# The tail of a four-head mixer stage: one projection moved up, one product moved back, one projection interleaved with broadcasts

## What is computed

```python
z = h @ w_in                               # columns: conv (x_c, B, C), q, k, v, o, gates
u = cg * xc                                # conv group, 512 channels, 4 tiles of 128
conv = w_conv[0]*full[:, 0:L] + w_conv[1]*full[:, 1:L+1] + w_conv[2]*full[:, 2:L+2]
y_conv = bg * conv
num = w_inter * (q C) + s v                # mLSTM, 4 heads of 128; s = (q k) * decay
den = w_inter * (q n) + sum(s)
h = num / max(|den|, exp(-mt))
C_new = w_old * C + sum(w_s k v)           # new state, an output; n_new alike
y = concat([group_rmsnorm(y_conv, 8), group_rmsnorm(sigmoid(o) * h, 4)]) @ w_out
x = x + gt1 * y
```

## Time and profile before

| | |
|---|---|
| median of three runs | 1788.6 us |
| runs | 1797.53, 1788.6, 1786.57 us |
| profiled execution | 1797.36 us, its span 1795.6 us |
| PE busy, share of the span | 1698.9 us, 95% |
| DVE, POOL, ACT busy | 1196.6, 1129.9, 666.7 us |
| mean granted TensorE clock | 0.976 of 2.4 GHz |

### The profile page before, as it was taken

The page is one execution under the profiler, slowest core; times in us unless marked ns, Lnnn a source line. Parts: engine busy times, 40 slices in busy tenths (PEclk is TensorE's granted clock), DMA queues, the critical chain, the costliest instruction groups (busy, mean ns, idle before and its releaser), DMA issues.

```text
span 1795.6 us, 27306 instructions
## 1 busy us (share of the span) xinstructions
PE 1698.9 (95%) x10559; PEld 1622.5 (90%) x10559; DVE 1196.6 (67%) x2286; ACT 666.7 (37%) x1063; POOL 1129.9 (63%) x676
## 2 busy tenths in 40 slices
PE   7999999798999999999999989888999999999996
PEld 3899887696999999999998989878999999999996
DVE  4341244625776799997777768455788787878855
ACT  2454232233334333323333333334444444444442
POOL 1667222031335897766666656586898899999862
PEclk9999999799999999999999999999999999999998
DMA  7545131224305888779998999999999999999961
GB/s 265 208 143 169 61 102 69 66 77 135 106 14 157 266 281 280 217 265 329 309 346 294 339 309 306 334 380 334 383 405 401 369 400 405 405 404 402 400 217 62
DMA packets 196737, 467.57 MB, mean 260 GB/s; under 512 B 21120, under 2 KB 103040, under 8 KB 196480
## 3 DMA queue, kind: packets, MB, share of 16 engines
q1 hardware_dynamic: 82176, 245.46, 38.8%
q0 software_dynamic: 46080, 167.79, 24.8%
q10 hardware_dynamic: 68352, 52.57, 9.0%
HBM read 410.78 MB, written 54.97 MB: 259 GB/s over the span
## 4 chain that ended last, share of the span: by engine, by line
PE 73%; DVE 10%; DMA 5%; ACTq 3%; POOL 3%; issue 3%; ACT 2%; SPq 0%; DVEq 0%; POOLq 0%
PE ps L886 41%; PE ps L672 18%; PE ps L897 4%; ACTq L1184 3%; PE ps L692 2%; DMA tab<-in_tab 2%; POOL tLo L630 2%; DMA ug<-in_urows,eidx 1%; DVE ug L1503 1%; PE ps L701 1%; POOL ug L640 1%; DVE best L1612 1%; PE ps L861 1%; DVE eqa L1605 1%; DVE eqb L1608 1%
## 5 line engine op out<-in xcount | busy, mean ns | idle before, releaser
L630 POOL TENSOR_TENSOR tLo<-tab,tHi 128x1024 fp32r<-128x1024 f32 x256 | 624.3, 2440 | 207.5 <-ACT tHi L1131 204.6
L886 PE MATMUL ps<-hHi,tLo 128*128 128x384 f32 x1024 | 357.0, 349 | 20.9 <-POOL tLo L630 13.7
L1131 ACT CAST tHi<-tab 128x1024 fp32r<-128x1024 f32 x256 | 268.3, 1048 | 290.1 <-PE ps L886 166.5
L886 PE MATMUL ps<-actHi,tLo 128*128 128x384 f32 x1024 | 343.1, 335 | 7.6 <-POOL tLo L630 4.2
L886 PE MATMUL ps<-hHi,tHi 128*128 128x384 f32 x1024 | 349.5, 341 | 0.0
L886 PE MATMUL ps<-hLo,tHi 128*128 128x384 f32 x1024 | 348.3, 340 | 0.0
L886 PE MATMUL ps<-actLo,tHi 128*128 128x384 f32 x1024 | 342.1, 334 | 0.0
L886 PE MATMUL ps<-actHi,tHi 128*128 128x384 f32 x1024 | 342.1, 334 | 0.0
L618 POOL TENSOR_TENSOR wLo<-raw,wHi 128x1024 fp32r<-128x1024 f32 x53 | 127.8, 2411 | 310.2 <-ACT wHi L967 310.2
L1503 DVE SCALAR_TENSOR_TENSOR ug<-ug,ps 128x1024 f32<-128x1024 f32 x160 | 192.1, 1218 | 88.0 <-DMA ug<-in_urows,eidx 86.7
L886 PEld LDWEIGHTS ps<-hHi,tLo 128*128 128x128 f32 x1024 | 196.4, 192 | 24.0 <-ACT ga L1181 14.6
(11 more groups left out here) (342 smaller groups left out, 2498.2 us busy)
## 6 DMA issues: line engine op xcount, KB each, us to landing
tab<-in_tab SPq DMA_DIRECT2D x256, 512.0 KB, 7.1
raw<-in_w SPq DMA_DIRECT2D x101, 512.0 KB, 3.9
gelu_scratch<-ga ACTq DMA_DIRECT2D x128, 192.0 KB, 5.0
gate_scratch<-stage ACTq DMA_DIRECT2D x12, 2048.0 KB, 17.8
gt<-gate_scratch SPq DMA_DIRECT2D x32, 768.0 KB, 7.7
gin<-gelu_scratch SPq DMA_DIRECT2D x128, 192.0 KB, 10.5
ug<-in_urows,eidx POOLq DMA_INDIRECT x160, 6.8
ug<-in_vrows,eidx POOLq DMA_INDIRECT x160, 7.7
```

What stands on the lines that cost most here:

```text
L630: pool.tensor_tensor(tLo[:, n % SPL], tab[:, n % TABS], tHi[:, n % SPL].bitcast(F32), ALU.subtract).then_inc(s_tlo, 1)
L886: last = mm(ps[:, bank, 0:TD], w, x[:, k, 0:TD], start=first, stop=end)
L1131: nc.scalar.copy(tHi[:, n % SPL], tab[:, n % TABS]).then_inc(s_thi, 1)
```

## The change

Three things are changed, and what hangs on them. First, in the table, units 26, 27 and 28 stand one place earlier: 26 behind the denominator of head 2, 27 behind its state product, 28 behind the transposes of head 3, and nothing in head 3 behind that. On DVE `conv(3)` moves from behind the weighted scores to ahead of the masks. Second, head 3's state product leaves its place behind the denominator, so that `group_sum(3)` follows the denominator; it now stands behind unit 29, in other banks, and its update on DVE behind the second residual of the output projection. Third, only two broadcasts stand ahead of unit 29; the other six stand inside it, broadcast k + 2 ahead of the matmuls of tile k, in two bank pairs in turn. The two small copies `cp` and `cs` move behind the sum of squares.

```diff
-AFTER_T, AFTER_S, AFTER_D, AFTER_ST = ([17, 21, 24, 27], [18, 22, 25, 28], [19, None, None, None], [20, 23, 26, None])
+AFTER_T, AFTER_S, AFTER_D, AFTER_ST = ([17, 21, 24, 28], [18, 22, 25, None], [19, None, 26, None], [20, 23, 27, None])
...
-            s = 2 * i if i < 2 else 4 + 2 * (i % 2)
+            s = 6 * (i % 2)
             return ps[:, s:s + 2, 0:HF]
...
-            def unit(n, free, made=None):
+            def unit(n, free, made=None, ahead=None):
...
                 for k in range(KT):
+                    if ahead is not None and k + 2 < KT:
+                        ahead(k + 2)
                     if made is not None:
                         pe.wait_ge(s_hlo, made + k + 1)
...
+            def group_rows_out(i):
+
+                if i >= 2:
+                    pe.wait_ge(s_y, i - 1)
+                rows = slice(0, 8) if i < CT else slice(32, GR)
+                for x in (grHi, grLo):
+                    for h in range(2):
+                        last = mm(bcast_pair(i)[:, h], bselr[rows, i % 4, :], x[rows, h * HF:(h + 1) * HF],
+                                  start=(x is grHi), stop=(x is grLo))
+                last.then_inc(s_gbc, 1)
...
+                if h < NH - 1:
+                    state_product(h, 2, (3, 4))
                 conv_unit(AFTER_ST[h])
 
             pe.wait_ge(s_ev, U_OUT)
             group_sum(NH - 1)
 
             pe.wait_ge(s_glo, 1)
+            group_rows_out(0)
+            group_rows_out(1)
+            unit(U_OUT, U_OUT, KT, group_rows_out)
+            pe.wait_ge(s_y, CT + NH)
+            state_product(NH - 1, 6, (4, 5))
+            for n in range(U_OUT + 1, U_PQ):
+                unit(n, max(n - 1, U_OUT))
             pe.wait_ge(s_stc, NH)
...
+                if h == NH - 1:
+                    conv(h)
                 v.wait_ge(s_ex, h + 1)
...
+                if k == 1:
+                    state_update(NH - 1, 6, (4, 5))
```

More of the change, by code:

```diff
@@ L763, in group_sum, with state_product @@
                 last.then_inc(s_gst, 1)
+            def state_product(h, small_bank, banks):
+                pe.wait_ge(s_vw, h + 1)
+                pe.wait_ge(s_hm, h + 1)
+                for i in range(NH):
+                    mm(ps[:, small_bank, 0:DH + 1], ktok[:, i, :], vw[:, i, :], start=(i == 0), stop=(i == NH - 1))
+                mm(ps[:, small_bank, 136:136 + NB], ktok[0:TS, NH, :], wsm[:], start=True, stop=True)
+                for i, b in enumerate(banks):
+                    last = mm(ps[:, b, :], ktok[0:TS, NH, :], vsm[:, 4 * i:4 * i + 4, :], start=True, stop=True)
+                last.then_inc(s_stp, 1)
+            def group_rows_out(i):
[7 more added lines that the diff above has]
+                last.then_inc(s_gbc, 1)
             for h in range(NH):
@@ L825, in _ @@
             pe.wait_ge(s_glo, 1)
-            pe.wait_ge(s_stc, NH)
[L827 to L837, removed]
+            group_rows_out(0)
[5 more added lines that the diff above has]
+                unit(n, max(n - 1, U_OUT))
+            pe.wait_ge(s_stc, NH)
             mod_rows(NMS)
@@ L1404, in group_add, with state_update @@
                 v.sem_inc(s_gacc, 1)
+            def state_update(h, small_bank, banks):
+                tt(nso[:, h], n0[:, h], wib[:, h, TS:TS + NB], ALU.mult)
+                link(tt(csb[:], csb[:], over(wib[:, h, TS:TS + NB], DH), ALU.mult))
+                v.wait_ge(s_stp, h + 1)
+                tt(csb[:, 0:4], csb[:, 0:4], ps[:, banks[0], :].rearrange("p (b d) -> p b d", b=4), ALU.add)
+                nc.vector.tensor_copy(cst[:, h], ps[:, small_bank, 0:DH])
+                nc.vector.tensor_copy(npo[:, h:h + 1], ps[:, small_bank, DH:DH + 1])
+                tt(nso[:, h], nso[:, h], ps[:, small_bank, 136:136 + NB], ALU.add)
+                tt(csb[:, 4:8], csb[:, 4:8], ps[:, banks[1], :].rearrange("p (b d) -> p b d", b=4), ALU.add).then_inc(s_stc, 1)
             for h in range(NH):
@@ L1443, in _ @@
                 v.wait_ge(s_den, h + 1)
[L1444 to L1453, removed]
+                last = tt(drow[32:GR, TP:T], drow[32:GR, TP:T], ps[32:GR, 5, 288:288 + TS], ALU.add)
                 if h < NH - 1:
+                    state_update(h, 2, (3, 4))
                     conv(h)
+                else:
+                    link(last)
             dp, dsm = drow[32:GR, 0:TP], drow[32:GR, TP:T]
```

6 lines of the change are left out of this document (2 added, 4 removed).

## The result

The changed kernel takes 1797.4 us, the median of 15 runs, beside 1789.7 us for the kernel before; the ratio is 1.0045 (95% interval 1.0027 to 1.0064), so 8.0 us slower, with 4.8 and 11.5 us as ends. Forecast was 0.3 us less than before. "Within 1%" holds, the direction does not.

The account below looks back on a forecast made before the run. PE, busy 95% of the span, bounds the kernel, so only its waits and half-clock time can go. Terms -3.5 (including -0.3) and +3.2 sum to -0.3 us: 1788.3 us from a 1788.6 median, range 1783 to 1801.

Parts of the forecast that it names:

- Parts 1 and 2: Units moved up, then head 3's numerator and denominator: longer numerator wait offsets the saved wait and state product, together -0.3 us.
- the collision: In conv(3) on DVE, one small instruction takes 2.32 us in place of 0.23, ending with POOL's subtraction; kept in forecast.
- Part 3: Broadcasts inside unit 29: clock rises 4.1 us after projection matmuls resume, unit ends at 357.3 against 360.85, -3.5 us including -0.3.
- The late bound: End of unit 29 if its tiles and broadcasts run at 1.2 GHz throughout: 362.5.
- The estimate by columns: Unit 29 at 2.4 GHz: 0.77 us a tile, 0.51 us a broadcast; 1.8 times that at 1.2 GHz.
- Part 4: Head 3's state product behind unit 29, wholly on PE's path ahead of unit 30: +3.2 us; later loads cost nothing.
- the limit: Loads of unit 35 on SP's queue were to start before 379 for the forecast to be right.
- The rival "the clock does not come back": Unit 29 stays at 1.2 GHz until the broadcasts are through: +6.7 us, 1795 us, up to 1801; chance 0.25.
- the point that was named to decide it: In unit 29, whether the granted clock is 1.00 before tile 5 decides if the clock comes back.

Follow-up runs that it names:

- e2: Kernel before with only the interleaving of broadcasts into unit 29; units, conv(3) and state product left in place: ratio 1.0014, +2.5 us.
- x1: Kernel before with 52 matmuls, results discarded, added in PE's wait for the group rows: ratio 0.9955, -8.1 us.
- a0: The changed kernel measured again, with nothing altered: ratio to before 1.0040, +7.2 us.
- e5: Changed kernel with head 3's state product moved from behind unit 29 into PE's wait for the group rows: ratio to before 1.0046, +8.2 us.
- e4: Changed kernel with 56 matmuls, results discarded, added in PE's wait for the group rows: ratio to before 1.0002, +0.4 us.
- e8: Changed kernel with 52 matmuls, results discarded, added in PE's wait for the group rows: ratio to before 0.9985, -2.7 us.
- e3: Changed kernel with broadcasts contracting 128 rows, zero-filled, in place of 8 or 4: ratio to before 0.9994, -1.1 us.
- b3: Changed kernel with 128-row broadcasts, state product in the group-row wait, conv(3) and head 2's group addition behind the weighted scores: ratio to before 0.9961, 1784.0 us.
- e6: Changed kernel with conv(3) on DVE put back behind the weighted scores: ratio to before 1.0035, +6.3 us.
- e7: Changed kernel with 128-row broadcasts and 56 matmuls, results discarded, in the wait for the group rows: ratio to before 0.9947, -9.5 us.
- b5: b3 with 30 matmuls, results discarded, added behind the state product in the wait: ratio to before 0.9879, 1771.4 us.
- b4: Changed kernel with 128-row broadcasts and the state product in the wait for the group rows: ratio to before 1.0000, 1791.3 us.
- e1: Changed kernel with all eight broadcasts put back ahead of unit 29, other two parts kept: ratio to before 1.0016, +2.9 us.
- x2: Changed kernel with 52 matmuls of 4 columns, results discarded, added at its very start: ratio to before 1.0114, +20.4 us.

## Why the prediction was wrong

- **Parts 1 and 2 held in their mechanism; that their balance did was partly luck.** The wait ahead of the numerator is 6.33 us (6.4 forecast), put down to the weighted scores, and the collision is there. DVE and POOL of the changed kernel:

```profile
316.53 2.33 DVE L1407 TENSOR_SCALAR xc<-us,vec 128x32 f32<-128x32 f32 x1
...
323.31 1.68 DVE L1461 TENSOR_TENSOR er<-er,ps 128x512 f32<-128x512 f32 x4
```

```profile
316.28 2.54 POOL L618 TENSOR_TENSOR wLo<-raw,wHi 128x1024 fp32r<-128x1024 f32 x1 [6.00 <-ACT wHi L981]
```

  The group sum takes 2.02 us, as forecast. The balance was put at -0.3 us and is +0.2 us: the clock came back 4.7 us behind the start of the numerator, where 3.5 us was taken and 4.1 us was the late bound. But the 1.8 us that the quicker group sum was counted for are no gain of the change in every execution, since e2 and x1, with the order of before, have a group sum of 2.02 us as well. Against those the balance is +1.8 us.
- **Part 3 failed, in the sentence "I take 357.3, because the granted clock rose inside this same unit before."** In before the clock rose behind 4 us of tiles without a broadcast among them. Inside the changed unit there is no such stretch before the last broadcast is through, and with contractions of 8 and 4 rows in turn with the tiles no rise came (change, a0, e2, e5); a clock that was up fell (e4, e8). Unit 29 took 22.68 us; forecast were 14.45 us (343.05 to 357.3, and 0.2). This one choice carries 8.2 us of a miss of 9.3 us in the stage. With 128 rows unit 29 takes 14.63 us, and the stage is 0.4 us from before where -0.3 was forecast. That 14.63 is so near 14.45 is partly luck: in e3 the clock is back ahead of tile 0, some 6 us sooner than the forecast had it, and the end is set by DVE, whose last low part the forecast had at 355.4 (12.4 us behind the first broadcast) and which came 13.5 us behind it.
- **The late bound was too early.** It had 362.5; unit 29 ended at 366.2 (366.0 in the span of before). The estimate by columns, times 1.8, gives 2.3 us for a broadcast and a tile at 1.2 GHz; the rows show 2.86 us. The first pair behind the change from 8 or 4 rows to 128, and the first behind the change back, take 0.82 us in place of 0.66, so that a broadcast lasts 1.20 us (349.12 to 350.32). b3, where all have 128 rows, takes 0.66 us for such pairs at the same 1.2 GHz (granted clock 0.50), and 2.27 us for a broadcast and a tile (340.17 to 342.44):

```profile
340.17 0.66 PE L795 MATMUL ps<-grHi,bwide 128*128 128x272 f32 x2
...
341.08 0.66 PE L685 MATMUL ps<-hHi,wLo 128*128 128x272 f32 x2
...
342.44 0.66 PE L795 MATMUL ps<-grHi,bwide 128*128 128x272 f32 x2
```

- **The rule of the Trainium skill ("TensorE: Matmul & The Clock Gate", Part 1), that activity releases the throttle,** was set against the row and rejected in the right direction, but not far enough. The trace disagrees with it for few-row matmuls in turn with tiles: PE busy for 19.7 of 20 us, and 0.50. It agrees for 128 rows in e3, with the clock back 3.3 us behind the first broadcast, but not in e6, where PE was busy for 10 of 10 us on numerator and denominator at 0.50.
- **Part 4 held.** The state product costs 3.7 us (3.2 forecast; its first 1.3 us were still at 1.2 GHz), and e5 shows that it was all on PE's path. SP's loads of unit 35 start at 384.58, later than the 379 that was named as the limit, since all is later; PE does not wait for them, so the term was rightly put at nothing. SP's queue of the changed kernel:

```profile
380.94 0.34 SPq L513 DMA_DIRECT2D out_C_s<-csb  x1
...
384.58 3.50 SPq L496 DMA_DIRECT2D raw<-in_w  x2
```

- **The rival "the clock does not come back" came true**, with its sign and near its size (+6.7 us; +9.0 in the stage). The nearness is partly luck, as its terms missed in opposite directions: it had unit 29 end 1.6 us later than before and 5.1 us for the state product, and the rows show 5.1 us and 3.7 us. It had a chance of 0.25, and the point that was named to decide it, the granted clock ahead of tile 5, decided it.

## What to carry to other kernels

To start waiting work earlier by mixing few-row matmuls into a projection cost the projection its clock here: a unit of 6.1 us at 2.4 GHz took nearly 19 us with six broadcasts in between. In this kernel such broadcasts were better contracted over all 128 rows with zeros (22.7 to 14.6 us for the same work), and the product that nobody waits for was better put into a wait than behind it (3.8 us of the stage; the run did not show it). When a forecast rests on the clock rising "as before", look at what ran in the microseconds ahead of that rise, and whether the change leaves that stretch whole. And before a term is read from one execution, look whether another execution of the same program has it.

## What the runs showed of the hardware

- Granted clock 0.50 over 20 us in which PE was busy for 19.7 us, when broadcasts of 8 and 4 rows alternated with 128-row tiles; with the same matmuls over 128 rows, most of them zeros, a clock that was at 1.00 stayed there (e7, b5) and one at 0.50 rose 3 to 9 us behind the first of them (e3, b4, b3). Broadcasts of 8 and 4 rows without tiles between them: 0.50 too (before, e1).
- The clock also fell in e6 behind a wait of only 2.88 us and stayed at 0.50 over 10 us with PE fully busy on numerator and denominator; behind a wait of 6.33 us in the change it was back after 4.7 us.
- In one execution of the same program the clock fell at about 329.7 and stayed at 0.50 for 6.8 us (before), in two others it did not fall there (e2, x1).
- At 1.2 GHz the first pair of matmuls behind a change of the row count takes 0.82 in place of 0.66 us. The same 0.82 us also stand without such a change where PE had to wait for DVE just before (before at 349.05, broadcast upon broadcast; the change at 363.34, tile upon tile).
- 52 matmuls of 128 rows and 4 columns, 104 instructions in the trace, took 22.35 us at the start of the program, 0.43 us each (x2), at a granted clock of 1.00, with 104 weight loads beside them; by their columns they had been taken for nothing.
